# A hybrid decoder step: the gates of two branches moved forward, key pages fetched earlier, eight value slots, and ScalarE doing the last tap of the short convolutions

## The reference, cut to what matters

```python
xn = rmsnorm(x); z = xn @ w_in              # one projection for all branches and gates
A: o_A = b * dwconv3(c * h)                 # short convolution
B: q,k,v = silu(dwconv4(g_q|g_k|g_v)); q,k l2-normalized
   S_t = a_t (I - b_t k_t k_t^T) S_(t-1) + b_t k_t v_t^T ; o_t = S_t^T q_t    # 4 heads, in chunks
   o_B = rmsnorm(o) * silu(g_z)
C: o_C = silu(layernorm(dwconv31(c_v * sigmoid(c_g)) + bias))
D: o_D = forgetting attention, 8 heads of 64; the samples also attend to 2048 paged past tokens
x += (sum_i sigmoid(gate_i) * (o_i @ w_branch[i])) @ w_out
x += cross_attention(rmsnorm(x)) @ w_co
x += (silu(dwconv3(rmsnorm(x) @ w_g)) * (.. @ w_u)) @ w_d
y = rmsnorm(x)
```

## Time and profile before

| what | us |
|---|---|
| median of 3 runs | 1827.02 |
| lowest, highest run | 1821.42, 1828.74 |
| the profiled execution's time | 1815.03 |
| its span, first to last instruction | 1813.2 |

### The profile page before, as it was taken

One profiled execution on the slowest core, in us unless ns is written; L12 is line 12 of the kernel. 1 busy time (PEld: TensorE's weight loads), 2 busy tenths in 40 slices (PEclk: granted clock), 3 DMA queues, 4 the chain that ended last, 5 costly groups with the idle time before them and its releaser, 6 DMA issues.

```text
span 1813.2 us, 28661 instructions
## 1 busy us (share of the span) xinstructions
PE 1541.0 (85%) x11204; PEld 1422.0 (78%) x11204; DVE 860.0 (47%) x1320; ACT 557.3 (31%) x906; POOL 637.6 (35%) x354
## 2 busy tenths in 40 slices
PE   7899899877586678899999467998588999999996
PEld 6899677666566678788888356987487999999996
DVE  4105877778886765423133033433513566663001
ACT  4333232244111322222222053343213333333222
POOL 3247344344466672222222012410402444443341
PEclk9999899888777889999999778999758999999998
DMA  6235232232345432455554425422312222222221
GB/s 202 95 100 187 69 110 79 82 117 88 105 118 181 131 123 83 147 167 172 184 165 145 127 65 210 155 93 94 116 35 63 90 94 94 94 94 89 89 97 48
DMA packets 158710, 208.32 MB, mean 115 GB/s; under 512 B 10468, under 2 KB 112413, under 8 KB 158168
## 3 DMA queue, kind: packets, MB, share of 16 engines
q1 hardware_dynamic: 139557, 173.65, 30.6%
q10 hardware_dynamic: 18027, 28.12, 4.5%
q0 software_dynamic: 992, 4.72, 0.8%
HBM read 192.08 MB, written 15.07 MB: 114 GB/s over the span
## 4 chain that ended last, share of the span: by engine, by line
PE 63%; DVE 18%; ACT 7%; issue 6%; DMA 3%; POOL 2%; SPq 1%; ACTq 0%; DVEq 0%; POOLq 0%
PE pb L823 45%; PE sd L823 15%; ACT ar L1162 3%; DVE ar L1691 3%; DVE ar L1551 2%; PE sd L827 2%; DVE ar L1571 1%; DVE ar L1557 1%; DVE ar L1698 1%; DVE ar L1554 1%; ACT L1162 1%; DMA ar<-in_cache_fox_v 1%; DMA ar<-in_cache_fox_k 1%; POOL ar L795 1%; SPq L683 1%
## 5 line engine op out<-in xcount | busy, mean ns | idle before, releaser
L784 POOL TENSOR_TENSOR wl<-raw,wh 128x1024 fp32r<-128x1024 f32 (+2 forms) x196 | 430.5, 2197 | 1026.5 <-ACT wh L1162 1025.1
L823 PE MATMUL pb<-xh,wh 128*128 128x260 f32 x2176 | 643.9, 296 | 22.2 <-DVE xl L1551 10.4
L823 PE MATMUL pb<-xl,wh 128*128 128x260 f32 x2176 | 626.7, 288 | 0.0
L823 PE MATMUL pb<-xh,wl 128*128 128x260 f32 x2176 | 625.0, 287 | 0.0
L823 PEld LDWEIGHTS pb<-xh,wh 128*128 128x128 f32 x2176 | 422.7, 194 | 38.9 <-issue 30.4
L823 PEld LDWEIGHTS pb<-xl,wh 128*128 128x128 f32 x2176 | 423.1, 194 | 0.5
L823 PEld LDWEIGHTS pb<-xh,wl 128*128 128x128 f32 x2176 | 422.5, 194 | 0.0
L1162 ACT ACTIVATE wh<-raw 128x1024 fp32r<-128x1024 f32 (+2 forms) x208 | 201.6, 969 | 587.8 <-PE pb L823 563.9
L823 PE MATMUL sd<-ar 128*128 128x128 f32 (+7 forms) x1584 | 277.4, 378 | 100.6 <-DMA ar<-in_cache_fox_v 24.6
L823 PEld LDWEIGHTS sd<-ar 128*128 128x128 f32 (+4 forms) x1584 | 197.4, 201 | 147.0 <-issue 99.9
L795 POOL TENSOR_TENSOR ar<-ar 128x512 f32<-128x512 f32 x128 | 179.0, 1399 | 96.3 <-DMA ar<-in_cache_fox_k 61.3
(11 more groups left out here) (173 smaller groups left out, 1792.1 us busy)
## 6 DMA issues: line engine op xcount, KB each, us to landing
raw<-in_w_in SPq DMA_DIRECT2D x40, 1024.0 KB, 5.4
ar<-in_cache_fox_k SPq DMA_DIRECT2D x128, 256.0 KB, 2.8
ar<-in_cache_fox_v SPq DMA_DIRECT2D x128, 256.0 KB, 3.0
raw<-in_w_ffn_in SPq DMA_DIRECT2D x22, 1024.0 KB, 5.1
raw<-in_w_branch SPq DMA_DIRECT2D x16, 512.0 KB, 3.5
raw<-in_w_ffn_out SPq DMA_DIRECT2D x8, 1024.0 KB, 5.0
gate_scratch<-ar ACTq DMA_DIRECT2D x16, 260.0 KB, 2.4
ar<-gate_scratch SPq DMA_DIRECT2D x16, 260.0 KB, 4.3
```

The costliest lines, as they stand in the source:

```text
L784: pool.tensor_tensor(wl[:, p % 2, 0:kt, :], raw[:, u % 2, 0:kt, half * P:(half + 1) * P], wh[:, p % 2, 0:kt, :].bitcast(F32), SUB).then_in ...
L823: return pe.matmul(o, l, r, start=start, stop=stop, skip_group_check=True)
```

## The change

The pieces of `gateD` and `gateB` move ahead of the pairs of A and C (to 44 to 59; A is then 60 to 75, C 76 to 91). The side list puts the first delta-rule chunk, `dc` and `ds` ahead of the end of the taps and of `cln`. A new step `fsq` makes the samples' query rows right after `fq`, so that the key pages start at piece 6 instead of 15. Taps run at one per half piece until `gateD`, then at two; key pages keep their rates. Values have eight slots (the old ring, and four places free by then), two semaphores by group, and loads two groups ahead; they start in piece 64 instead of 68. The values' row buffer is single. `cln` uses other scratch. In the short convolutions ScalarE writes the last tap from PSUM with the tap's weight as its scale, and the samples' past positions are multiplied and summed once for all tiles (at the first), to be added by one small step for a tile.

```diff
     for n in range(6):
         unit("w_in", 0, KD, C_GQ + n * 256, "gx", 2 * n)
+    for br in "DB":
+        for h in range(4):
+            unit("w_in", 0, KD, C_GATE + "ABCD".index(br) * D + h * 256, "gate" + br, 2 * h)
     for br in "AC":
...
-    for br in "DB":
-        for h in range(4):
-            unit("w_in", 0, KD, C_GATE + "ABCD".index(br) * D + h * 256, "gate" + br, 2 * h)
...
-TAPS_TICK, K_EARLY, K_LATE = 2, 1, (2, 2)
+TAPS_TICK, K_TICK = (1, 2), (1, 2)
...
-        + [("AFTER", "fq")] + [("sm", n) for n in range(4)]
+        + [("AFTER", "fq")] + [("fsq", n) for n in range(2)] + [("KSTART",)] + [("sm", n) for n in range(4)]
         + [("AFTER", "fv")]
-        + [("fst", n) for n in range(4)] + [("KSTART",)]
+        + [("fst", n) for n in range(3)]
...
-        + [("TAPS",)]
-        + [("cln", n) for n in range(7)] + [("BEFORE", "gateC")]
         + [("gdn", n, 0) for n in range(-1, 12)]
         + [("REDUCES",)]
         + [("gdn", n, 0) for n in range(12, 18)]
         + [("dc", n) for n in range(3)] + [("ds", n) for n in range(4)] + [("VSTART",)]
+        + [("TAPS",)]
+        + [("cln", n) for n in range(7)] + [("BEFORE", "gateC")]
...
-            if g + 1 < N_VG:
-                out.append(("vload", g + 1))
+            if g + 2 < N_VG:
+                out.append(("vload", g + 2))
...
-            background("tap", TAPS_TICK)
-            background("k", K_EARLY if p < first_piece("gateA") else K_LATE[h])
+            background("tap", TAPS_TICK[p >= first_piece("gateD")])
+            background("k", K_TICK[p >= first_piece("gateD")])
...
+        vring = [v(DEC + 512 * n, 512) for n in range(4)] + [cols[:, B_GS:B_GS + 4, :].rearrange("p a b -> p (a b)"), v(SQ, 512), v(SQ + 512, 512), v(PR + 4 * T + 527, 512)]
...
-                sp.dma_start(kring[:, i % 4, :], a[cache][bass.ds(n, 1)].rearrange("a p l h d -> (a p) (l h d)"))\
-                    .then_inc(page_in[i % 4], 16)
+                k = cache == "cache_fox_k"
+                sp.dma_start(kring[:, i % 4, :] if k else vring[i % 8], a[cache][bass.ds(n, 1)].rearrange("a p l h d -> (a p) (l h d)"))\
+                    .then_inc(page_in[i % 4] if k else v_in[i // V_GROUP % 2], 16)
...
+                    sp.wait_ge(pe_s.sem, upto(pe_works, ITEMS.index(("ds", 1)) + 1))
+                    for i in range(V_GROUP, 2 * V_GROUP):
+                        page("cache_fox_v", i)
                 elif e[0] == "vload":
-                    sp.wait_ge(v_used.sem, e[1])
+                    sp.wait_ge(v_used.sem, e[1] - 1)
...
-                for j in range(V_GROUP):
-                    pe.wait_ge(page_in[j], 16 * (N_PAGE // 4 + g + 1))
+                pe.wait_ge(v_in[g % 2], 16 * V_GROUP * (g // 2 + 1))
...
                 elif kind == "cg" or kind.startswith("gate"):
+                    if kind == "gateA" and idx < 2:
+                        act.wait_ge(gate_out[s], 16 * KD)
...
-                    fn(both(cb[:, s, 3:3 + T]), x, ACT.Copy, mt_act)
+                    act_c.by(act.activation(both(cb[:, s, 3:3 + T]), x, ACT.Copy))
+                    if kind == "gx" and idx == 0:
+                        act.wait_ge(pe_s.sem, upto(pe_works, ITEMS.index(("fvt", 4))))
+                    if kind == "gx" and idx >= 4:
+                        at = ITEMS.index(("fox", 8 * (idx % 4) + 9 if idx == 4 else FOX - 1))
+                        act.wait_ge(pe_s.sem, upto(pe_works, at + 1))
+                    w = col(V_GW + 36 + idx) if kind == "gx" else cols[:, B_FW, 2 * KF + idx:2 * KF + idx + 1]
+                    fn(both(gx_tile(idx) if kind == "gx" else pairA[:, s, :]), x, ACT.Copy, mt_act, scale=w)
...
-                    if b >= 2:
-                        act.wait_ge(v_picked.sem, b - 1)
-                    fn(vrow[:, b % 2, :], s3, ACT.Copy, v_rows)
+                    if b >= 1:
+                        act.wait_ge(v_picked.sem, b)
+                    fn(vrow, s3, ACT.Copy, v_rows)
...
+            def past_sums(rows, w, dst, width, n):
+
+                prod = tmp[:, 0:NB * width * n].rearrange("p (q b r) -> p q b r", q=4, b=2)
+                tt(prod, rows, w[:, None, None, :].to_broadcast([P, 4, 2, width * n]), MUL)
+                red(dst, tmp[:, 0:NB * width * n].rearrange("p (b j r) -> p b r j", b=NB, j=width), ADD)
+
+            def short_conv(x, y, width, wcol, past):
+
+                dve_c.by(dve.tensor_tensor(y[:, SEQ:T], y[:, SEQ:T], past, ADD))
+                for j in range(width - 1):
+                    if j:
+                        dve.wait_ge(dve_c.sem, dve_c.n)
+                    (ev_y if j == width - 2 else dve_c).by(dve.scalar_tensor_tensor(
+                        out=y[:, 0:SEQ], in0=x[:, 4 - width + j:4 - width + j + SEQ], scalar=wcol(j), in1=y[:, 0:SEQ], op0=MUL, op1=ADD))
...
-                    conv(cb[:, s, :], gx_tile(idx), GCW, lambda j: col(V_GW + 12 * j + idx), hist, col(V_GW + 36 + idx), ev_y)
+                        past_sums(gh, cols[:, B_VEC, V_GW:V_GW + 36], gpast, 3, 12)
+                    short_conv(cb[:, s, :], gx_tile(idx), GCW, lambda j: col(V_GW + 12 * j + idx), gpast[:, :, idx])
```

More of the change, by code:

```diff
@@ L489, in build @@
         tmp = v(PR + 4 * T + 1048, T)
+        gpast = cols[:, B_GS, 0:12 * NB].rearrange("p (b r) -> p b r", b=NB)
+        fpast = cols[:, B_FS:B_FS + 2, :].rearrange("p a b -> p (a b)")[:, 0:KF * NB].rearrange("p (b r) -> p b r", b=NB)
+        csq, clr = pairA[:, 0, :], pairA[:, 1, :]
         sm_at = [SM]
@@ L540, in build @@
         page_in = [sem(f"page_in{n}") for n in range(4)]
+        v_in = [sem(f"v_in{n}") for n in range(2)]
         qb_in, xs_out, xs_in, qs_out = sem("qb_in"), sem("xs_out"), sem("xs_in"), sem("qs_out")
@@ L974, in side @@
                     last = mm(s2[:, 16:32], ones, gtok[:, :, :].rearrange("p a b -> p (a b)"))
-                elif kind == "fst" and n < 3:
-                    if n == 0:
-                        pe.wait_ge(mt_act.sem, mt_a[mt_of("fv")])
+                elif kind in ("fsq", "fst"):
+                    j = n + (kind == "fst")
+                    pe.wait_ge(mt_act.sem, mt_a[mt_of("fv" if j else "fq")])
                     for c in range(4):
-                        last = tr(s0[0:NB, c * P:(c + 1) * P], fs[:, 4 * n + c, :])
+                        last = tr(s0[0:NB, c * P:(c + 1) * P], fs[:, 4 * j + c, :])
                 elif kind in ("fvt", "fkt") and n < QT:
@@ L1041, in side @@
                     for c in (range(KB) if n == 0 else [n - 1] if n < 5 else []):
-                        src = oC[:, c, :] if n == 0 else lsq
+                        src = oC[:, c, :] if n == 0 else csq
                         for h in range(2):
-                            last = mm(sd[:, (0 if n == 0 else 2) + h, 0:TH], ones, src[:, h * TH:(h + 1) * TH], c == 0, c == KB - 1)
+                            last = mm(sd[:, h, 0:TH], ones, src[:, h * TH:(h + 1) * TH], c == 0, c == KB - 1)
                 elif kind == "gs":
@@ L1126, in pages @@
                     pe.wait_ge(v_num.sem, g // V_PER)
[L1127 to L1128 removed]
+                pe.wait_ge(v_in[g % 2], 16 * V_GROUP * (g // 2 + 1))
                 lhs = sc[:, V_GROUP * g:V_GROUP * (g + 1), :].rearrange("p i h -> p (i h)")
                 for j in range(V_GROUP):
[L1131 removed]
+                    last = mm(s3[32 * j:32 * j + 32, :], lhs, vring[V_GROUP * (g % 2) + j], g % V_PER == 0, g % V_PER == V_PER - 1)
                 v_used.by(last)
@@ L1137, in picked @@
                 for c in range(KB):
-                    last = mm(s3[:, c * FH:(c + 1) * FH], vrow[:, b % 2, c * P:(c + 1) * P], pick)
+                    last = mm(s3[:, c * FH:(c + 1) * FH], vrow[:, c * P:(c + 1) * P], pick)
                 v_picked.by(last)
@@ L1306, in side @@
                     fins = act.activation(rsum[:, 0:1], eps6[:, 0:1], ACT.Copy)
+                elif kind == "fsq":
+                    fn(srow[0:NB, 1, :], s0[0:NB, :], ACT.Copy)
+                    store(qscr, srow[0:NB, 1, :], qs_out)
+                    fins = act.activation(rsum[:, 0:1], eps6[:, 0:1], ACT.Copy)
                 elif kind == "fst":
-                    if n == 3:
+                    if n == 2:
                         act.wait_ge(qs_out, 16)
-                    fn(srow[0:NB, n % 2, :], s0[0:NB, :], ACT.Copy)
-                    if n == 1:
-                        store(qscr, srow[0:NB, 1, :], qs_out)
-                    else:
-                        dst = out["fk_s" if n == 2 else "fv_s"]
-                        store(dst.rearrange("b t l h d -> b (t l h d)"), srow[0:NB, n % 2, :], ss_st)
+                    fn(srow[0:NB, (n + 1) % 2, :], s0[0:NB, :], ACT.Copy)
+                    dst = out["fk_s" if n == 1 else "fv_s"]
+                    store(dst.rearrange("b t l h d -> b (t l h d)"), srow[0:NB, (n + 1) % 2, :], ss_st)
                     fins = act.activation(rsum[:, 0:1], eps6[:, 0:1], ACT.Copy)
@@ L1385, in side @@
                             act.wait_ge(v2a.sem, va + 1)
```

(8 more changed lines are left out.)

29 lines of the change are left out of this document (11 added, 18 removed).

## The result

The changed kernel takes 1753.89 us (median of 4 runs, 1751.12 to 1757.37) where the kernel before took 1827.88 us in runs beside it: a ratio of 0.960, 95% interval 0.957 to 0.963. The forecast was 1739 us, in a range of 1698 to 1786. The profiled execution of the new kernel has a span of 1750.1 us, 63.1 us less than before, where the sum of terms said 88. The missing 25 us show only as 15 in the forecast, because the profiled execution of before lay 12 us under its median and that of after lies 2 us under its own; that part of the closeness is luck.

The account below looks back on a forecast made before the run. Bound by stretch: TensorE at 798–962 us, VectorE at 345–459, mutual waits at 459–652, value loads in the tail. Terms summed to 88 us gained, 1727 us; with 12 us for the runs' median, 1739 us, range 1698 to 1786.

Parts of the forecast that it names:

- four signs of a right forecast: No value-load waits before `brD`; ScalarE's `gx` wait well under 43 us; pieces 32–43 about 30 shorter; pre-`gz` sixteen near 143.
- the `gx` stretch: 345 to 459 us: VectorE loses 31.7 us of work, TensorE becomes the bound; gain 26 us (12 to 31).
- Pieces 76 to 91: 798 to 962 us, TensorE-bound: 192 fewer matmuls save 23 us, 2 given back; gain 21 us (12 to 23).
- Pieces 44 to 59: Hand-over gains 12 us, new order in pieces 46 to 51 gains 2, pieces 52 to 59 lose 7.
- the hand-over: 459 to 503 us: TensorE idles 15.3 us because of VectorE's backlog, most of it gone; gain 12 us (0 to 15).
- the term of the early keys: At the start, a query-row wait moves in and weight loads stand behind page loads; loss 4 us (0 to 8).
- Pieces 60 to 67: Layer norm and 14 taps come in, part of the chunk and the keys leave; 0 us, 10 either way.
- Attention: 161 to 299 us: half-rate taps take 22 taps off VectorE; gain 4 us (0 to 9).
- the tail: 1012 to 1050 us: eight value slots, earlier start and loads two groups ahead gain 29 us (24 to 33).
- The collision: Rival, chance 0.2: 46 late taps collide with GpSimd at 2.04 us each, 43 us in all, giving 1782 us.
- The clock rival: Rival, chance 0.2: TensorE's clock stays up from 345 to 652 us, 30 us more gained, giving 1709 us.
- The slow chunk behind the keys: Rival, chance 0.06: pieces 44 to 56, state steps wait behind taps and keys; loss 122 us, ending at 1861 us.

## Why the prediction was right, and where it was not

The direction and the range hold; of its four signs of a right forecast only the first holds, nearly, and the second in part. Value loads before `brD`: one wait of 2.1 us is left. ScalarE's wait for VectorE in the `gx` tiles: 31.0 us for 43.4, less than "well under". Pieces 32 to 43: 9.8 us shorter, not 30. The sixteen pieces before `gz`: 156.3 us, not 143. None of the signs of a wrong one came: pieces 44 to 59 took 184.2 us, taps 1.25 us, and GpSimd has no wait for pages at the start.

**The step that failed: the `gx` stretch**, "Then PE at 83.3 us is the bound", a gain of 26 us; it was 7.5, under my lower bound of 12. Of the 31.7 us that were to leave VectorE 21.4 did: the taps (20.4) and the passes (6.3) went as forecast, but the small add took 891 ns, not 304, and each pass that stayed 953 ns, not 820. The wrong inference was that the engine with most work, 95.3 of 114 us, was what TensorE waited for. I had read ScalarE's wait for VectorE but not TensorE's own in that stretch: 18.6 of its 25.9 idle us were for the norm's scaling step. Shown by three runs: 15 taps more cost 2.8 us, all taps off give 2.3, and the norms moved out give 19.2, of them 10.3 TensorE's idle time, at the same load of VectorE.

**Pieces 76 to 91**, a gain of 21, was 16.5 with the matmuls that stand in the `gz` row: mis-sized in what I gave back. All the 192 matmuls went (193 records, 21.6 us of busy time for 23), and TensorE's idle time grew by 5.1 us (13.8 to 18.95), where I gave back 2. The doubled matmuls show the price, and that the matmuls used to cover 2.9 of the 5.1 us; the rest is open.

**Pieces 44 to 59** (12 and 2 less 7, so 7) gained 9.3. By halves they seem to miss both ways, 2.6 for 14 and 6.7 for −7, but that is the cut: the forecast's times after, 100 and 87 us, came out as 97.8 and 86.4. The reasons held less well than the times. Pieces 44 to 47, where the hand-over lies, gained 5.2 us (53.7 to 48.5), not 12, and the wait of 10.9 us is still 6.2. TensorE's idle time in pieces 44 to 51 fell by 7.1 us (29.8 to 22.7), and its busy time rose by 4.5: the wide pieces' matmuls did not all go into idle time, as I had them. VectorE is as busy as before there (87.3 of 98 us), because the taps taken from the `gx` tiles arrive here; without any taps the eight pieces take 88.4. In pieces 52 to 59, VectorE's 23.5 us of waiting for key products read now, from 536.5 to 622.9 us:

```profile
DVE ar L1723 <- POOL ar L805: 2.4, 3, 1.2
```

The run with late keys shows that this comes with the early start (114.1 us instead of 86.4), so the term of the early keys, −4, belongs together with this one. **Pieces 60 to 67** lost 7.8, inside the 10 given; the run with the old order shows the layer norm of C in it.

**Attention** was larger than taken, 8.6 for 4 (the upper bound was 9); the tail was 28.6 for 29, with its waits for values gone as foreseen. The terms that fell short miss by 35 us together (`gx` 18.5, pieces 60 to 67 7.8, 76 to 95 4.5, 68 to 75 3.7, the tail 0.4); attention gives 4.6 back, pieces 44 to 59 2.3 and small ones 3.1, which leaves the 25.

**The rivals.** The collision did not come as priced: its 43 us would have come from 46 taps alone, at 2.04 us each for the 1.10 of the forecast; the mean was 1.25, and all 120 taps together cost 26 us. The rule of the Trainium skill (SBUF — State Buffer, "Who interferes with whom") agrees with a mean of 1250 ns where the median tap took 752, as before. Most of the taps' time lies beside other work. The clock rival came in part, inside the forecast: pieces 44 to 51 and 52 to 59 ran at 0.81 and 0.94 of the clock, where they had 0.70 and 0.82 before; the `gx` pieces stayed at 0.86 (0.87). The slow chunk behind the keys did not come with this change, but does when the keys start late: that one wait of 24 us is its mechanism.

**The parts**, each undone alone, are worth 28 us (early keys), 29 (two groups ahead), 32 (order and tap rate) and 5 (ScalarE's tap), 94 in all for a change of 74: they overlap.

## What to carry to other kernels

Before the busiest engine of a stretch is called its bound, list what the engine on the critical path waits for in that stretch, by line: work taken off an engine gains only what these waits give back. A step that is moved is worth what it does at both places: each of the norms, the keys and the taps gained in one stage and was paid for in another. When two edits remove matmuls and keep a serial chain beside them, count the chain's steps that the matmuls used to hide.

## What was not expected of the hardware

The profile shows two table loads of 1283 ns in each norm, one ahead of the logarithm and one ahead of the exponential, eight in the `gx` stretch (10.3 us). The Trainium skill (ScalarE: Activation LUTs, "Table sets: the hidden batching unit") counts one load for a logarithm followed by an exponential, since one set holds both; here each had its own, and the rows decide. The same page of the Trainium skill ("What ACT_TABLE_LOAD costs") gives that 1283 ns and adds a drain of about 1380 ns; in the timeline above the next instruction begins 0.02 us after the load. With one load less in each of four norms, 5.1 us (4 times 1.28) would leave this chain: an estimate, not tried.

In the attention stretch 17.5 us of extra VectorE work cost 12.7 us, though VectorE was full in neither run (107.9 of 141.3 us with the taps, 90.9 of 128.6 without), and only 5.1 of them are idle time of TensorE. The other 7.65 are the same matmuls taking longer, at a granted clock of 0.94 for 1.00: part of the stretch ran at the lower of the two levels, 1.2 GHz. I read this as the price of the idle gaps. Their sum alone does not set it: with late keys the same pieces have the change's idle time (2.98 us), a granted clock of 0.99, and 1.5 us more busy time.
